# A two-layer hybrid decoder trunk: the input slab goes first in the first recurrence group, its low products come last, and two small preparations are shared out anew

## The reference

```python
def hgrn2_chunked(q, f_logit, i, lb):
    f = lbb + (1.0 - lbb) * jax.nn.sigmoid(to_chunks(f_logit))
    k = 1.0 - f
    qc, vc = to_chunks(q), to_chunks(i)
    b = jnp.cumsum(jnp.log(f), axis=3)
    q_dec = qc * jnp.exp(b)
    k_inv = k * jnp.exp(-b)
    att = jnp.where(causal, jnp.einsum('bhncd,bhnsd->bhncs', q_dec, k_inv), 0.0)
    o_intra = jnp.einsum('bhncs,bhnsv->bhncv', att, vc)
...
def rotary(x, pos, rot_dim, theta):
    inv = theta ** (-jnp.arange(half, dtype=jnp.float32) / half)
    ang = pos.astype(jnp.float32)[..., None] * inv
    cos = jnp.cos(ang)[:, :, None, :]
    sin = jnp.sin(ang)[:, :, None, :]
```

## Time and profile before

| | us |
|---|---|
| median of three runs | 581.52 |
| the profiled execution, its time | 581.78 |
| its span | 579.8 |
| TensorE busy | 571.3 |
| VectorE busy | 435.5 |
| ScalarE busy | 392.5 |
| GpSimd busy | 72.0 |

### The profile page before, as it was taken

How to read it: one execution, slowest core, us unless ns; L and a number is a source line. 1 busy time by engine, 2 the same in 40 slices (tenths; PEclk the granted TensorE clock), 3 DMA queues, 4 the chain that set the end, 5 groups by cost and what they waited for, 6 DMA issues and landing times.

```text
span 579.8 us, 8803 instructions
## 1 busy us (share of the span) xinstructions
PE 571.3 (99%) x3364; PEld 504.6 (87%) x3364; DVE 435.5 (75%) x683; ACT 392.5 (68%) x600; POOL 72.0 (12%) x77
## 2 busy tenths in 40 slices
PE   8999999999999999999999999999999999999995
PEld 7999989888888888888888889999889988888984
DVE  6879689688847874568757896799998974876663
ACT  6863784596657575557666858969759837566754
POOL 4130005039101000100000001111110100100002
PEclk9999999999999999999999999999999999999999
DMA  9856355556953544564345545326544563356201
GB/s 292 257 181 229 102 189 194 170 159 193 272 167 100 200 146 145 185 230 167 145 146 167 196 158 203 122 102 235 199 146 146 182 234 139 116 204 231 93 1 73
DMA packets 51854, 98.82 MB, mean 170 GB/s; under 512 B 1733, under 2 KB 7141, under 8 KB 51813
## 3 DMA queue, kind: packets, MB, share of 16 engines
q1 hardware_dynamic: 50628, 96.95, 49.1%
q0 software_dynamic: 1024, 1.05, 0.8%
q10 hardware_dynamic: 160, 0.27, 0.1%
HBM read 96.16 MB, written 1.05 MB: 168 GB/s over the span
## 4 chain that ended last, share of the span: by engine, by line
PE 97%; DMA 1%; DVE 1%; ACT 0%; issue 0%; SPq 0%; DVEq 0%; ACTq 0%
PE proj L1972 18%; PE proj L1996 11%; PE proj L1997 11%; PE proj L1998 11%; PE proj L1973 9%; PE proj L1955 6%; PE proj L1957 6%; PE proj L1956 6%; PE head L2212 4%; PE proj L1977 3%; PE proj L1976 1%; PE head L2290 1%; PE head L2056 1%; DMA x_residual<-in_x_dram 1%; PE head L2189 1%; PE head L2257 1%
## 5 line engine op out<-in xcount | busy, mean ns | idle before, releaser
L1177 DVE TENSOR_TENSOR w_lo<-raw_weights,w_hi 128x1024 fp32r<-128x1024 f32 x174 | 222.1, 1288 | 86.8 <-ACT w_hi L548 83.1
L548 ACT ACTIVATE w_hi<-raw_weights 128x1024 fp32r<-128x1024 f32 x174 | 182.4, 1056 | 109.4 <-PE proj L1998 48.9
L1972 PE MATMUL proj<-xT,w_hi 128*128 128x512 f32 x392 | 142.0, 401 | 0.0
L1973 PE MATMUL proj<-xT,w_lo 128*128 128x256 f32 x392 | 109.8, 280 | 0.0
L1955 PE MATMUL proj<-xT,w_hi 128*128 128x256 f32 x304 | 87.3, 287 | 0.0
L1972 PEld LDWEIGHTS proj<-xT,w_hi 128*128 128x128 f32 x392 | 73.7, 188 | 15.4
L1957 PE MATMUL proj<-xT,w_lo 128*128 128x256 f32 x304 | 86.0, 283 | 0.0
L1956 PE MATMUL proj<-xT,w_hi 128*128 128x256 f32 x304 | 86.0, 283 | 0.0
L1973 PEld LDWEIGHTS proj<-xT,w_lo 128*128 128x128 f32 x392 | 74.0, 189 | 1.8
L1996 PE MATMUL proj<-w_hi,y 128*128 128x512 f32 x176 | 69.4, 395 | 0.0
L1998 PE MATMUL proj<-w_lo,y 128*128 128x512 f32 x176 | 68.6, 390 | 0.0
(11 more groups left out here) (328 smaller groups left out, 920.4 us busy)
## 6 DMA issues: line engine op xcount, KB each, us to landing
raw_weights<-in_ev_w_in_dram SPq DMA_DIRECT2D x15, 2048.0 KB, 9.1
raw_weights<-in_od_w_in_dram SPq DMA_DIRECT2D x12, 2048.0 KB, 7.9
raw_weights<-in_ev_w_out_dram SPq DMA_DIRECT2D x4, 2048.0 KB, 7.8
raw_weights<-in_xa_wkv_dram SPq DMA_DIRECT2D x4, 2048.0 KB, 8.3
raw_weights<-in_od_w_out_dram SPq DMA_DIRECT2D x4, 2048.0 KB, 7.8
raw_weights<-in_xa_wq_dram SPq DMA_DIRECT2D x2, 2048.0 KB, 9.1
raw_weights<-in_xa_wo_dram SPq DMA_DIRECT2D x2, 2048.0 KB, 7.7
x_residual<-in_x_dram SPq DMA_DIRECT2D x2, 512.0 KB, 3.9
```

The costliest lines, as they stand in the source:

```text
L548: act.activation(ring_quarter(w_hi, n, q), raw_quarter(n, q), ACT.Copy).then_inc(hi_ready, 1)
L1177: dve.tensor_tensor(ring_quarter(w_lo, n, q), raw_quarter(n, q), ring_quarter(w_hi, n, q).bitcast(F32), ALU.subtract).then_inc(lo_ready, 1)
L1972: pe.matmul(both, wh[:, k, :], x[:, :, k, :], start=(k == 0), stop=False)
L1973: pe.matmul(dst[:, 0:S], wl[:, k, :], x[:, 0, k, :], start=False, stop=False)
```

## The change

- `SLABS`: in the first group slab i stands ahead of slab f. In the second group nothing moves.
- Loads: slab i of the first group comes in six pieces by k (four of 256 KB, two of 512 KB, semaphores `first_landed`), slab f of the first group in four column quarters of 512 KB (`second_landed`), where it was the first slab before, in two quarters and a half.
- `low_last` is TensorE's code for the first slab: for each pair of k first the products of the high weights with `xT_hi` and then `xT_lo`, each as soon as its own part is there, and the products of the low weights behind them. GpSimd casts the weights of k = 0, VectorE makes their low part and both parts of k = 1. The first product no longer waits for `xT_lo`.
- The last part of the row scaling (half a row of the second tile, `row_half(1, 1)`) goes from VectorE to ScalarE (`row_cols`, `rows_shared`).
- The v rows of the first group are copied ahead of the gate work, and the calls of `ahead` around them move.
- The angles of both rotations stand in one tile (`angle`), the one of 64 frequencies on the partitions 0 to 63, the other above; VectorE's steps run over 256 elements instead of 512, and four sines of ScalarE on 64 partitions spread them to `trig`.

```diff
+SLABS += [("A", "i", "T", 0), ("A", "f", "F", 0), ("A", "q", "F", 0), ("A", "z", "X", 0)]
+SLABS += [("A", "f", "F", 1), ("A", "i", "T", 1), ("A", "q", "F", 1), ("A", "z", "X", 1)]
...
+        angle = memT[:, 4:6, :]
...
+            for c, (k, n_k) in enumerate(((0, 1), (1, 1), (2, 1), (3, 1), (4, 2), (6, 2))):
+                sp.dma_start(raw[:, 0, :].rearrange("p (k c) -> p k c", k=KC)[:, k:k + n_k, :],
+                             dram_slab(0)[:, k:k + n_k, :]).then_inc(first_landed[c], 16)
...
+            for q in range(4):
+                sp.dma_start(raw_quarter(1, q), dram_slab(1)[:, :, P * q:P * q + P]).then_inc(second_landed[q], 16)
...
-            pool.wait_ge(first_hi, 2)
-            pool.tensor_tensor(ring_quarter(w_lo, 0, 0), raw_quarter(0, 0), ring_quarter(w_hi, 0, 0).bitcast(F32),
-                               ALU.subtract).then_inc(first_lo, 1)
...
             act.wait_ge(prm_turned, 1)
             act.activation(prm[:, 0:KC], proj[2][:, 0:KC], ACT.Copy).then_inc(prm_ready, 1)
-            act.wait_ge(first_landed[0], 16)
-            act.activation(ring_quarter(w_hi, 0, 0)[:, 0:2, :], raw_quarter(0, 0)[:, 0:2, :], ACT.Copy).then_inc(first_hi, 1)
+            act.wait_ge(row_factored, 2)
+            act.activation(row_cols(mem_rows, 1, 1), row_cols(x_sb, 1, 1), ACT.Copy, scale=st[:, 7:8]).then_inc(rows_shared, 1)
             act.drain()
-            xT_high(0, 0, "ev_norm", 0)
-            act.wait_ge(first_landed[1], 16)
+            xT_high(0, 0, "ev_norm", 0, range(0, 4))
+            act.wait_ge(first_landed[2], 16)
+            act.wait_ge(first_landed[3], 16)
             act.activation(ring_quarter(w_hi, 0, 1), raw_quarter(0, 1), ACT.Copy).then_inc(hi_ready, 2)
+            xT_high(0, 0, "ev_norm", 0, range(4, 8))
+            i0 = slab("A", "i", 0)
             ahead(-1, 3)
-            ahead(slab("A", "f", 0), 0)
+            for q in range(3):
+                ahead(i0, q)
+            for t in range(T):
+                filled(act, i0, t)
+                act.activation(v_sb[:, t, :], bank(i0, t)[:], ACT.Copy).then_inc(v_ready, 1)
+                act.drain().then_inc(free_of(i0, t), 1)
             act.preload_act_table(ACT.Exp)
             act.wait_ge(prm_turned, 2)
-            act.activation(prm[:, KC:N_EARLY], proj[2][:, KC:N_EARLY], ACT.Copy).then_inc(prm_ready, 1)
+            act.activation(prm[:, KC:N_EARLY], proj[3][:, KC:N_EARLY], ACT.Copy).then_inc(prm_ready, 1)
+            ahead(i0, 3)
...
+                    ahead(i, 2)
+                    ahead(i, 3)
+                else:
+                    ahead(q, 0)
+                    act.wait_ge(prm_turned, 3)
+                    act.activation(prm[:, N_EARLY:], head[0][:, N_EARLY:N_ROWS], ACT.Copy).then_inc(prm_ready, 1)
                 act.wait_ge(b_ready, g + 1)
                 act.activation(wview(0), wview(2), ACT.Exp, scale=-1.0).then_inc(exps_ready, 1)
                 act.activation(chunk_decay[:], chunk_sum[:], ACT.Exp).then_inc(exps_ready, 1)
                 act.activation(wview(3), wview(2), ACT.Exp).then_inc(exps_ready, 1)
-                ahead(q, 0)
-                v_rows(i)
-                if g == 0:
-                    act.wait_ge(prm_turned, 3)
...
-                    act.activation(trig[:], trig[:], ACT.Sin).then_inc(trig_ready, 1)
+                    for w in range(2):
+                        for a in (0, 64):
+                            last = act.activation(trig[a:a + 64, 2 * w:2 * w + 2, :], angle[64 * w:64 * w + 64, :, :],
+                                                  ACT.Sin)
...
-            row_half(1, 1)
-            dve.wait_ge(first_landed[0], 16)
-            dve.tensor_copy(ring_quarter(w_hi, 0, 0)[:, 2:4, :], raw_quarter(0, 0)[:, 2:4, :]).then_inc(first_hi, 1)
+            def first_low(k):
+
+                dve.wait_ge(first_hi[k], 1)
+                dve.tensor_tensor(first_rows(w_lo, k), raw_quarter(0, 0)[:, k, :], first_rows(w_hi, k).bitcast(F32),
+                                  ALU.subtract).then_inc(first_lo, 1)
+
+            first_low(0)
+            dve.wait_ge(first_landed[1], 16)
+            dve.tensor_copy(first_rows(w_hi, 1), raw_quarter(0, 0)[:, 1, :]).then_inc(first_hi[1], 1)
             dve.wait_ge(prm_ready, 1)
-            xT_low(0, "ev_norm", 0)
-            dve.wait_ge(first_lo, 1)
+            xT_low(0, "ev_norm", 0, range(0, 2))
+            first_low(1)
+            xT_low(0, "ev_norm", 0, range(2, 4))
             dve.wait_ge(hi_ready, 2)
             dve.tensor_tensor(ring_quarter(w_lo, 0, 1), raw_quarter(0, 1), ring_quarter(w_hi, 0, 1).bitcast(F32),
                               ALU.subtract).then_inc(lo_ready, 2)
+            xT_low(0, "ev_norm", 0, range(4, 8))
+            i0 = slab("A", "i", 0)
...
+            def low_last(n, q):
+
+                wh, wl = ring_quarter(w_hi, n, q), ring_quarter(w_lo, n, q)
+                for k in (2 * q, 2 * q + 1):
+                    pe.wait_ge(xT_hi_ready, k + 1)
+                    if q == 0:
+                        pe.wait_ge(first_hi[k], 1)
+                    else:
+                        pe.wait_ge(hi_ready, q + 1)
+                    for x, ready in ((xT_hi, xT_hi_ready), (xT_lo, xT_lo_ready)):
+                        pe.wait_ge(ready, k + 1)
+                        for t in range(T):
+                            pe.matmul(bank(n, t)[:], x[:, k, P * t:P * t + P], wh[:, k % 2, :],
+                                      start=(k == 0 and ready is xT_hi_ready), stop=False)
+                if q == 0:
+                    pe.wait_ge(first_lo, 2)
+                else:
+                    pe.wait_ge(lo_ready, q + 1)
+                for t in range(T):
+                    for k in (2 * q, 2 * q + 1):
+                        last = pe.matmul(bank(n, t)[:], xT_hi[:, k, P * t:P * t + P], wl[:, k % 2, :],
+                                         start=False, stop=(k == KC - 1))
+                    if t == 0 and q == 3:
+                        last.then_inc(first_tile_filled, 1)
                 last.then_inc(quarter_used, 1)
 
...
-                    first_slab(f)
-                    slab_t(i)
+                    first_slab(i)
+                    pe.wait_ge(prm_ready, 1)
+                    slab_f(f, [0, 1])
+                    pe.wait_ge(prm_ready, 2)
+                    slab_f(f, [2, 3])
                     late_params()
                     slab_f(q)
```

142 lines of the change are left out of this document (57 added, 85 removed).

## The result

The changed kernel takes 583.97 us in the median of 22 runs (582.4 to 585.44), the kernel before, run beside it, 582.21 (581.39 to 584.45, 22 runs). The ratio is 1.0031 with an interval of [1.0022, 1.0039]: **1.8 us, 0.3%, slower**. It lies outside the range of 580.7 to 583.2 on record. The profiled executions say the same: 583.88 us (span 582.2) against 581.78 (span 579.8). The upper end of the scatter goes with the granted clock: of 97 runs of the kernel before that stood beside the experiments, the 16 above 583.3 us have a mean clock of 0.994 to 0.996 and all others but one have 0.997 to 0.999; three runs far outside, 707.5 and 707.6 us of the kernel before and 951.0 us of experiment 7, have 0.75 and 0.56 and are in no ratio.

What follows compares the result with a forecast made beforehand. TensorE, busy 99% of the span, was taken as the bound. Gain 1.05 against new wait 0.3 + 0.1 + 0.75 + 0.3 = 1.45: net 0.4 us longer, 581.9 us against a median of 581.52; range 580.7 to 583.2.

Steps and rivals of the forecast that it cites:

- The start: Opening: first product needs only xT_hi(0), so it moves from 9.61 to 9.05; gain 0.55 us, bounds 0 to 0.75.
- The end of the two slabs: Slabs i and f on TensorE end at 32.1 instead of 33.13.
- The gain: Start and first two slabs together: 1.05 us gained, bounds 0.7 to 1.3.
- The chain's own excess: Gates to qdec, before the head products: 15.1 against 14.82 us, wait 0.3, plus 0.1 for slab q's w_lo.
- GpSimd's hold of the third low part: GpSimd's carried-key product delays VectorE's third w_lo of slab z: 0.75 us of wait, bounds 0 and 1.3.
- The angles: Rotations side by side: about 1.1 us more for ScalarE, nothing on the path, 1.6 us of cover.
- the last term of the new wait, slab q's load: Slab q's load, issued at 17 to 20, reaches ScalarE's first cast 0 to 2.4 us late; 0.3 taken.
- the second rival: Slab q's load held behind short runs, 1.5 to 2.4 us late, wait 3.1, time 583.5; chance 0.14.
- Its bound: Second rival: slower from 1.9 us of total lateness of the chain on.
- one stop, ahead of the head products: Sign to look for: TensorE waits 0.5 to 2 us before the head products, put down to VectorE's qdec.
- the low part of slab z's first quarter: VectorE's w_lo, ready 11.5 us after f and wanted at 11.99; a wait for it would show the forecast wrong.

Runs made afterwards that it cites:

- experiment 7: Changed kernel with the angles as before (double-width VectorE steps, one ScalarE sine pass): 584.27 us, ratio 1.0034.
- experiment 4: Changed kernel, twelve small loads behind slab q's load, GpSimd's carried products held until both halves of q_dec are made: 581.69 us, ratio 0.9989.
- Experiments 1 and 2: Both on the changed kernel. 1: one load for slab f instead of four, 581.74 us. 2: twelve small loads behind slab q's load, 582.38 us.
- experiment 3: Changed kernel, twelve small loads behind slab q's load, low part of slab z's third quarter behind both q_dec halves: 581.12 us, ratio 0.9980.
- experiment 9: Kernel before, with slab q's load held until ScalarE has split slab i's first quarter: 582.43 us, ratio 1.0006.
- experiment 10: Changed kernel with one load for f and third low part behind q_dec, slab q's load held for slab f's first low part: 581.81 us, 0.9989.
- experiment 5: Changed kernel with one load for slab f and the low part of slab z's third quarter behind both q_dec halves: 580.62 us, ratio 0.9976.

## Why the prediction was wrong

**Right, and at its size.** The start: first product forecast at 9.05, at 9.02 in the profile. The end of the two slabs: forecast 32.1, seen 32.10. The gain: forecast 1.05, measured 1.02. That these dates agree so closely is partly luck: the same opening started anywhere from 8.88 to 9.83. Counted from ScalarE's pass over the second tile of x (5.58 before, 5.44 after) the first product came 0.45 us sooner, not 0.59, so 0.14 of the 1.02 belongs to that execution. From the first product to slab f's end 23.05 was forecast and 23.08 measured (23.52 before). The chain's own excess, forecast 0.3 + 0.1: 0.30 in experiment 4. GpSimd's hold of the third low part, forecast 0.75: 0.66. The Trainium skill, SBUF — State Buffer, "Who interferes with whom", says that the engine that starts first keeps the shared ports for its whole instruction; the 1.86 us that become 1.21 in experiment 4, and 1.52 on the next step, agree. The angles: forecast at nothing, and nothing that can be told in experiment 7.

**The step that failed** is the last term of the new wait, slab q's load: "0 to 2.4 us late", of which I took 0.3. The mechanism was named and its size was wrong, 2.0 in place of 0.3. Slab q's load was issued at 18.92, inside the 17 to 20 that I had put, and its first cast came 2.1 us late. Already the middle of my own issue range gives 18.5 + 9.1 - 26.6 = 1.0 of lateness; and this load took 9.75 us from its issue to that cast, not 9.1. Experiments 1 and 2, which take that lateness away by two different means, shorten the stretch by 2.0 and 1.8 us. With 2.0 in place of 0.3 the forecast of the stretch, 38.34 + 0.56 for the earlier start + 0.4 = 39.3, becomes 41.0 (measured 40.87), and the time 583.6. The measured terms close the account: -1.02 + 0.30 + 0.66 + 2.0 = 1.94, the lateness of the head products. The late load was the second rival's mechanism, and its 583.5 is near the 583.97 measured, though the comparison's median of before was itself 0.7 above the three runs shown: it had 2.0 us of loss, 1.8 were measured. (Its bound is off: with 1.05 gained, a loss of 1.16 needs 2.2 us of wait and not 1.9.)

**Why I sized it so low.** I argued that the bytes are the same in all. Bytes were not what held the queue: the same 2 MB held it for 0.40 us in experiment 1. Twelve small loads need 5.3 us of SyncE's queue (13.59 to 18.87), and they stand behind 8.0 us of column loads. The trace of before had rows for both, the half slab with runs of 1 KB and the last of the same twelve small loads, which began at 8.53:

```profile
2.81 2.68 SPq L382 DMA_DIRECT2D raw_weights<-in_ev_w_in_dram  x1
...
15.28 0.43 SPq L391 DMA_DIRECT2D memT<-in_positions_dram  x1
```

So 1 MB held the queue for 2.68 us there, and the twelve small loads for 7.2. From twice 2.68 behind 5.5, and 7.2 more, an estimate of the issue is 18.1, and with 9.1 to the landing a lateness of 0.6; I didn't add it up. The 8.0 us themselves, with runs half as long, stand in no row of before. The rate of the short runs was 290 GB/s again, beside 397 with 2 KB, so the row of the Trainium skill, DMA: Bandwidth & Descriptors, Specifications, by which 512 bytes are enough for line rate, does not hold in this case. The rate alone cost nothing that can be told: the stretch is 37.90 with the short runs (experiment 3) and 37.91 without (experiment 5).

**Also missed: where lateness shows.** I expected one stop, ahead of the head products, and took the low part of slab z's first quarter to be ready 0.5 us before it is wanted. It would have been. Two us of lateness use that up, and stops appear at every handover from VectorE on the way: 1.01, 0.32 and 1.02. In sum they are the lateness once (2.0) and the chain's excess of 0.96, 3.0 us, not three times over, since TensorE's own delay at one stop shortens the next.

**What the change does, then.** The new opening as a whole (order, low products last, row half) is shorter by 1 us; no experiment takes its parts apart but the row half. The order i, f instead of f, i also takes away the 10.9 us of slab i's products between the gate's input and slab q. The old order absorbs without a trace the 1.8 us for which slab q's cast waited (experiment 9), the new one passes on 1.4 of 1.9 (experiment 10), although that kernel already has the shorter chain. With slab q's load in time and the third low part out of the chain, the same order is faster than the kernel before by 1.1 us.

## What to carry to other kernels

When a reorder brings a dependent chain closer to its consumer, first add up the slack that it spends, and then check each load that feeds the chain for its issue time, not only its bandwidth: sum the queue from its front, every short descriptor and every small load included. Small loads that nobody needs soon belong behind the next large load, and work on VectorE that nobody on the chain needs belongs behind the chain's step. An undone part that costs nothing (here the angles and the row half) may be covered by another loss: test it again once that loss is gone. To compare edits of a fraction of a per cent, find the stretch in which they act and measure that: here the rest of the kernel repeated within 0.3 us while whole runs scattered by 3.
